# Attention's bias, sinks and first tiles loaded one stage earlier, in an encoder layer on one Trainium2 core

## The chip, the cores and the metric

The kernel runs on one core of one Trainium2 chip. A core has five instruction streams that meet only through semaphores: TensorE (PE, matrix products and transposes), VectorE (DVE), ScalarE (ACT), GpSimd (POOL) and SyncE (SP, which in this kernel issues nearly all DMAs). The metric is the device time of one launch in microseconds (us); lower is better. Three runs of the kernel before gave 1611.4, 1613.11 and 1617.85 us, so the median is 1613.11.

## The reference, cut to what matters

One encoder layer is computed for two token sets that share weights: 1024 sample tokens and 512 prompt tokens, all float32.

```python
h = rmsnorm(x); qa, ka, va, qb, kb, vb = split(h @ w_in)      # 8 heads of 64 in each group, 2 key/value heads
A: s = q.k*scale + bias(rel), |q-k| <= 128; m = max(s, sink); p = exp(s-m)/(sum exp(s-m) + exp(sink-m)); o = p @ v
B: q, k rms-normalised per head and rotated; p = softmax(q.k*scale) over all keys; o = p @ v
x += concat(rmsnorm(oA), rmsnorm(oB)) @ w_out
x += expert_choice_moe(rmsnorm(x)); x += sigmoid(rmsnorm(x) @ w_pg) * (p @ w_pp); y = rmsnorm(x)
```

## The kernel before, in words

The program is a chain of stages, each a block of the five streams: the projection (`project_inputs`), attention on the sample tokens (`attend`, stage name `sample`), attention on the prompt tokens (`attend` again, stage name `prompt`), output product and routing, experts, and the last product. A stage ends when its SP stream has seen its last stores land; then semaphores are cleared and all engines meet at a barrier (`Arena.give_back`, L65-L69). No instruction of a stage is issued before that barrier, so whatever a stage reads from DRAM begins to move only then.

Tokens go in 12 tiles of 128: 8 of the sample, 4 of the prompt. Each float32 operand is held as a high and a low part. The projection writes, for every tile, q (transposed, high and low, 1 MB), k (512 KB) and v (128 KB) to the DRAM arrays `qT_d`, `kT_d` and `v_d` (`store`, L238-L248). `qT` and `kT` in SBUF are single buffers: ACT's `copy_out` of tile t waits until the stores of tile t-1 have landed (L349-L353). Early in the stage `w_raw`, a ring of three, holds raw weights until DVE has made their low parts, and ACT stores the table of relative biases, spread over all partitions, to `rel_d` (L151-L153). SP's order in this stage is written out: x tile t+1 in, q, k, v of tile t-2 out.

`attend` goes through n tiles. In each, PE makes the scores of 16 heads (0 to 7 group A: a span of two or three blocks of keys in `ka`; 8 to 15 group B: all keys of the token set, in `kb`), DVE finds the maxima (in group A it adds `bias` first, L963), ACT takes the exponentials (L909), PE transposes the probabilities (L807) and multiplies with `va` or `vb` (L817). `q`, `ka` and `va` have two slots, by the parity of the tile. PE's head 0 of a tile waits for q, ka and va of its slot (L774-L776), head 8 of the first tile waits for `kb` and `vb` (L777-L778), and DVE begins with `nsinks`, after `bias` and `sinks` have landed (L1031-L1032). An identity matrix for the transposes is made by POOL at the start of each stage (L74-L81), and PE waits for it first. SP's queue after the barrier is

```python
load(0, 0, True, False)                    # q, ka, va of the first tile
if tile0 == 0: consts.load(sp)             # bias 1536 KB, sinks
sp.dma_start(kb[:]...); sp.dma_start(vb[:]...)
load(1, 1, False, False)                   # q, ka, va of the second tile
if tile0 == 0: consts.load_gains(sp)
if w: w.load(sp, w_next, 0, KC // 2)       # prompt stage alone: half of w_out
```

The prompt stage reuses `bias`, `sinks` and the gains `g_mix`, and beside its own work splits `w_out` for the next stage (ACT L103, DVE L107, from head 11 of its first tile on).

Of the kernel before, what the change touches and what calls it, by code (L numbers as in the profile page):

```python
# [6 lines left out]
F32 = mybir.dt.float32  # L7
# [33 lines left out]
class Arena:  # L41
# [7 lines left out]
    def sb(self, name, shape, dt=F32):  # L49
        return self.ctx.enter_context(self.nc.sbuf_tensor(f"{self.stage}_{name}", shape, dt))  # L50
# [20 lines left out]
    def sems(self, name, n):  # L71
        return [self.sem(f"{name}{i}") for i in range(n)]
# [82 lines left out]
def project_inputs(nc, x, w_in, g_attn, gqk, rope, rel_bias, hot, outside, qT_d, kT_d, v_d, rel_d):  # L155
# [3 lines left out]
    with ExitStack() as ctx:  # L159
        a = Arena(nc, ctx, "proj")  # L160
        sb, sem, sems = a.sb, a.sem, a.sems
        w_raw = sb("w_raw", [P, RING, QKV])
        w_hi = sb("w_hi", [P, KC, QKV], F32R)
        w_lo = sb("w_lo", [P, KC, QKV], F32R)
        ident, ident_r = sb("ident", [P, P]), sb("ident_r", [P, P], F32R)
# [28 lines left out]
        p_qk = a.ps("p_qk", [P, 2, 4, P])  # L194
        bias = BiasRows(a)

# [24 lines left out]
        def _(sp):  # L221
# [46 lines left out]
            sp.wait_ge(bias.stored, 16)  # L268
# [302 lines left out]
class AttentionConsts:  # L571


    def __init__(self, nc, kept, rel_d, sink, g_mix):
        self.rel_d, self.sink, self.g_mix = rel_d, sink, g_mix
        tensor = lambda name, shape: kept.ctx.enter_context(nc.sbuf_tensor(name, shape, F32, side="right"))
        self.bias = tensor("bias", [P, HEADS, SPAN])
        self.sinks = tensor("sinks", [P, HEADS])
        self.g_all = tensor("g_mix", [P, 2, HEADS * HD])
        self.landed, self.gains_landed = kept.sem("landed"), kept.sem("gains_landed")  # L580

    def load(self, sp):
# [8 lines left out]
def attend(nc, stage, tile0, n, qT_d, kT_d, v_d, consts, mixed_d, w_next=None, out_w=None):  # L591
# [7 lines left out]
    with ExitStack() as ctx:  # L599
# [3 lines left out]
        bias, sinks, g_all = consts.bias, consts.sinks, consts.g_all  # L603
        nsinks = sb("nsinks", [P, HEADS])
        nhalf = sb("nhalf", [P, 1])
        q_sb = sb("q", [P, 2, 2 * HEADS, P], F32R)
        ka = sb("ka", [P, 2, 2 * KV, SPAN], F32R)
        va = sb("va", [P, 2, 3, KV * HD])
        kb = sb("kb", [P, 2 * KV, T], F32R)
        vb = sb("vb", [P, n, KV * HD])  # L610
# [23 lines left out]
        kb_landed, q_landed, w_landed = sem("kb_landed"), sems("q_landed", 2), sems("w_landed", 2)  # L634
# [57 lines left out]
        def _(sp):  # L692
            tok = tile0 * P

            def load(i, s, first, last):
# [8 lines left out]
                sp.dma_start(q_sb[:, s].bitcast(F32).rearrange("p h q -> p (h q)"), qT_d[src(row, P), :]).then_inc(  # L704
                    q_landed[s], 16)
                start = left + lo * P
                sp.dma_start(ka[:, s, :, lo * P:hi * P].bitcast(F32),
                             kT_d[:, 0:2 * KV, src(start, (hi - lo) * P)]).then_inc(w_landed[s], 16)
                sp.dma_start(va[:, s, lo:hi, :],
# [11 lines left out]
            load(0, 0, True, False)  # L721
            if tile0 == 0:
                consts.load(sp)
            sp.dma_start(kb[:].bitcast(F32), kT_d[:, 2 * KV:, tok:tok + T]).then_inc(kb_landed, 16)
            sp.dma_start(vb[:], v_d[tok:tok + T, 0:KV * HD].rearrange("(b p) d -> p b d", p=P)).then_inc(
                kb_landed, 16)
            load(1, 1, False, False)
            if tile0 == 0:
                consts.load_gains(sp)
# [15 lines left out]
            step(n - 2, 0, last=True)  # L745
            for i in (n - 2, n - 1):
                store(i, A)
                store(i, B)
# [20 lines left out]
        def _(pe):  # L769
            def scores(i, s, head, first, last):  # L770
# [15 lines left out]
                if head < HEADS:  # L786
                    parts = [(slice(lo * P, hi * P), [ka[:, s, 2 * kv + f, lo * P:hi * P] for f in range(2)])]
                else:
                    parts = [(slice(c, c + BANK), [kb[:, 2 * kv + f, c:c + BANK] for f in range(2)])
                             for c in range(0, T, BANK)]  # L790
                for cols, (k_hi, k_lo) in parts:
                    pe.matmul(p_s[:, slot, cols], q_sb[:, s, h, :], k_hi, start=True, stop=False)  # L792
                    made = pe.matmul(p_s[:, slot, cols], q_sb[:, s, h, :], k_lo, start=False, stop=True)  # L793
# [16 lines left out]
            def values(s, g, blocks, begin, end):  # L810


                for b in blocks:
                    for kv in range(KV):
                        v = (va[:, s, b, kv * HD:(kv + 1) * HD] if g == A else vb[:, b, kv * HD:(kv + 1) * HD])
# [134 lines left out]
        def _(dve):  # L950
# [80 lines left out]
            dve.wait_ge(consts.landed, 32)  # L1031
# [5 lines left out]
            dve.wait_ge(consts.gains_landed, 16)  # L1037
# [1100 lines left out]
def encoder_layer(nc, i, y):  # L2138
# [12 lines left out]
    with ExitStack() as ctx:  # L2151
# [4 lines left out]
        project_inputs(nc, i["x"], i["w_in"], i["g_attn"], i["gqk"], i["rope"], i["rel_bias"], i["hot"],  # L2156
                       i["outside"], qT_d, kT_d, v_d, rel_d)
        with ExitStack() as both:
            held = Arena(nc, both, "attend")
            consts = AttentionConsts(nc, held, rel_d, i["sink_a"], i["g_mix"])  # L2160
            attend(nc, "sample", 0, SAMPLE_TILES, qT_d, kT_d, v_d, consts, mixed_d)
# [5 lines left out]
            attend(nc, "prompt", SAMPLE_TILES, TILES - SAMPLE_TILES, qT_d, kT_d, v_d, consts, mixed_d, i["w_out"], out_w)  # L2167
# [60 lines left out]
```

## Time and profile before

| | us |
|---|---|
| median of three runs | 1613.11 |
| the profiled execution | 1608.08 |
| its span, first to last instruction | 1606.3 |
| PE busy | 1442.6 (90% of the span) |
| DVE, ACT, POOL busy | 932.2, 723.0, 182.1 |
| projection's last engine instruction ends; sample stage's first score | 269.8; 282.6 |
| sample stage's last PE work; prompt stage's first score | 560.6; 574.0 |

In the rows, times are in us from the span's start and durations in us, or in ns where a mean is given. A row of a timeline names the start, the duration, the engine, the line, the operation, the tensor written and those read, and in brackets how long the engine was idle before and what ended that. "SPq" rows are DMAs being issued; the bytes move afterwards. PEclk is the clock that TensorE was granted, 1.00 being 2.4 GHz and 0.50 being 1.2 GHz.

### The profile page before, as it was taken

What the parts mean: (1) busy time and instruction counts of PE and PEld (TensorE: products, weight loads), DVE (VectorE), ACT (ScalarE), POOL (GpSimd) and SP (SyncE); (2) the same over time, 40 slices, a digit from 0 to 9 for tenths busy, and PEclk for the clock granted to TensorE, in tenths of its full rate; (3) what the DMA queues carried; (4) which work ended last, traced back from release to release, by engine and by line L of the source; (5) the groups of instructions that cost most, each with busy time, mean ns of one, the idle gap of its engine ahead of it and who ended that gap; (6) DMA issues with size and microseconds to landing.
All of it is one profiled execution on the core that took longest, in us unless ns stands there. A gap on an engine that the chain in (4) does not pass through costs nothing. (4 is left out here: it accounts for less than half of the span.)

```text
span 1606.3 us, 21541 instructions
## 1 busy us (share of the span) xinstructions
PE 1442.6 (90%) x7320; PEld 1015.2 (63%) x7320; DVE 932.2 (58%) x1324; ACT 723.0 (45%) x1157; POOL 182.1 (11%) x255
## 2 busy tenths in 40 slices
PE   5899996799999869689998779999999999938997
PEld 4788885555565445368887556666666666627885
DVE  5454443677777557622257756676676676644553
ACT  4344433666677557522222444544544544423332
POOL 1111110000000000000001211121121121021110
PEclk9899998799999979889998979999999999978998
DMA  8533324621111063064441846778788788753331
GB/s 259 95 112 111 111 98 165 225 71 64 64 64 62 21 236 115 33 220 135 157 144 66 300 164 214 261 261 266 257 259 265 259 261 265 247 158 119 131 132 66
DMA packets 118847, 261.53 MB, mean 163 GB/s; under 512 B 7648, under 2 KB 37472, under 8 KB 115720
## 3 DMA queue, kind: packets, MB, share of 16 engines
q1 hardware_dynamic: 110592, 233.55, 41.4%
q0 software_dynamic: 7168, 25.17, 6.6%
q10 hardware_dynamic: 1032, 2.10, 1.1%
q8 instruction: 32, 0.52, 0.1%
q14 instruction: 23, 0.19, 0.0%
HBM read 194.20 MB, written 66.58 MB: 162 GB/s over the span
## 5 line engine op out<-in xcount | busy, mean ns | idle before, releaser
L1751 DVE TENSOR_TENSOR moe_w_lo<-ring,moe_w_hi 128x2048 fp32r<-128x2048 f32 x96 | 220.3, 2295 | 162.9 <-ACT moe_w_hi L1690 162.9
L1690 ACT ACTIVATE moe_w_hi<-ring 128x2048 fp32r<-128x2048 f32 x96 | 183.7, 1914 | 207.3 <-PE moe_p_g L1873 78.1
L1422 PE MATMUL mix_p_big<-kept_out_w,mix_m_hi 128*128 128x512 f32 x384 | 126.2, 410 | 4.6 <-DVE mix_m_lo L1297 2.4
L519 PE MATMUL proj_p_out<-proj_w_hi,proj_h_hi 128*128 128x512 f32 x264 | 109.8, 416 | 8.4 <-DVE proj_qn L418 8.4
L1881 PE MATMUL moe_p_gu<-ring,moe_xT_r 128*64 128x512 f32 x512 | 116.9, 598 | 0.0
L519 PE MATMUL proj_p_out<-proj_w_lo,proj_h_hi 128*128 128x512 f32 x264 | 105.1, 398 | 0.0
L519 PE MATMUL proj_p_out<-proj_w_hi,proj_h_lo 128*128 128x512 f32 x264 | 104.9, 397 | 0.0
L971 DVE TENSOR_REDUCE sample_ntop<-sample_p_s 128x1 f32<-128x1024 f32 x64 | 78.1, 1222 | 37.9 <-PE sample_p_s L793 37.2
L807 PEld LDWEIGHTS sample_p_t<-sample_ident_r,sample_probs_r 128*128 128x128 f32 x688 | 73.0, 141 | 23.4 <-ACT sample_probs L909 6.7
L1422 PEld LDWEIGHTS mix_p_big<-kept_out_w,mix_m_hi 128*128 128x128 f32 x384 | 72.8, 195 | 21.3 <-issue 2.6
L807 PE MATMUL sample_p_t<-sample_ident_r,sample_probs_r 128*128 128x128 f32 x688 | 80.3, 246 | 5.0 <-ACT sample_probs L909 2.5
L2126 PE MATMUL tail_p_out<-kept_pg_hi,tail_h_hi 128*128 128x512 f32 x192 | 77.5, 404 | 2.4 <-DVE tail_h_lo L2072 2.4
L909 ACT ACTIVATE sample_probs<-sample_p_s,sample_ntop 128x1024 f32<-128x1024 f32 x64 | 71.4, 1116 | 18.1 <-DVE sample_ntop L971 17.7
L1422 PE MATMUL mix_p_big<-kept_out_w,mix_m_lo 128*128 128x512 f32 x192 | 77.6, 404 | 0.0
L2126 PE MATMUL tail_p_out<-kept_pg_hi,tail_h_lo 128*128 128x512 f32 x192 | 76.6, 399 | 0.0
L2126 PE MATMUL tail_p_out<-kept_pg_lo,tail_h_hi 128*128 128x512 f32 x192 | 76.2, 397 | 0.0
L1881 PEld LDWEIGHTS moe_p_gu<-ring,moe_xT_r 128*64 128x64 f32 x512 | 33.9, 136 | 66.1 <-issue 66.1
L792 PE MATMUL sample_p_s<-sample_kb,sample_q 128*128 128x512 f32 x128 | 57.7, 451 | 9.1 <-ACT sample_probs L909 8.6
L817 PE MATMUL sample_p_o<-sample_pT_b,sample_vb 128*64 128x512 f32 x256 | 62.9, 606 | 0.8 <-ACT sample_pT_b L896 0.8
L1649 POOL DMA_INDIRECT acc_d<-ring,kept_slots x32 | 50.5, 1579 | 96.2 <-DVE ring L1792 92.0
L519 PEld LDWEIGHTS proj_p_out<-proj_w_hi,proj_h_hi 128*128 128x128 f32 x264 | 50.0, 189 | 17.8 <-issue 8.5
L909 ACT ACTIVATE sample_probs<-sample_s_a,sample_ntop 128x384 f32<-128x384 f32 (+1 forms) x64 | 37.6, 588 | 46.7 <-DVE sample_ntop L967 45.5
(298 smaller groups left out, 3141.5 us busy)
## 6 DMA issues: line engine op xcount, KB each, us to landing
ring<-in_w_gate SPq DMA_DIRECT2D x32, 1024.0 KB, 5.8
ring<-in_w_up SPq DMA_DIRECT2D x32, 1024.0 KB, 7.6
ring<-in_w_down SPq DMA_DIRECT2D x32, 1024.0 KB, 7.2
qT_d<-proj_qT SPq DMA_DIRECT2D x12, 1024.0 KB, 3.9
sample_q<-qT_d SPq DMA_DIRECT2D x8, 1024.0 KB, 5.1
proj_x<-in_x SPq DMA_DIRECT2D x12, 512.0 KB, 4.3
proj_w_raw<-in_w_in SPq DMA_DIRECT2D x8, 768.0 KB, 5.8
kT_d<-proj_kT SPq DMA_DIRECT2D x12, 512.0 KB, 3.6
```

The source lines that it names most:

```text
L519: last = pe.matmul(p_out[:, cols], h[:, s, k, :], w[:, k, cols], start=(k == 0 and n == 0), stop=(k == KC - 1 and n == 2))
L792: pe.matmul(p_s[:, slot, cols], q_sb[:, s, h, :], k_hi, start=True, stop=False)
L807: last_mm = pe.transpose(p_t[:, bank, b, :].bitcast(F32R), probs_r[:, head % 4, at:at + P], ident_r[:])
L817: mm = pe.matmul(p_o[kv * HD:(kv + 1) * HD, :, :], v, pT[:, b, kv, :, :], start=(b == begin), stop=(b == end - 1))
L909: act.activation(dst, src, ACT.Exp, bias=ntop[:, s, head:head + 1], accum_out=total[:, s, head:head + 1]).then_inc(exp_done, 1)
L971: dve.tensor_reduce(ntop[:, s, head:head + 1], p_s[:, head % 2, 0:T], AX.X, ALU.max, negate=True).then_inc(ntop_done, 1)
L1422: mm = pe.matmul(p_out[:, cols], m[:, s, k, :], ww[:, k, cols], start=(k == 0 and n == 0), stop=(k == KC - 1 and n == 2))
L1649: pool.indirect_dma_start(out=acc_d, out_offset=bass.IndirectOffsetOnAxis(ap=slots[0:rows, col:col + 1], axis=0), in_=y, in_offset=None, c ...
L1690: act.activation(w_hi[:, at % SPLIT], raw[:, at % RAW], ACT.Copy).then_inc(hi_made, 1)
L1751: dve.tensor_tensor(w_lo[:, at % SPLIT], raw[:, at % RAW], w_hi[:, at % SPLIT].bitcast(F32), ALU.subtract).then_inc(lo_made, 1)
L1881: mm = pe.matmul(out[half * R:(half + 1) * R, :], x[:, k0 + k, :], raw[:, (at + half) % RAW, k, :], start=(start and k == 0), stop=(stop a ...
L2126: mm = pe.matmul(p_out[:, s, cols], h[:, s, k, :], ww[:, k, cols], start=(k == 0 and n == 0), stop=(k == KC - 1 and n == 2))
```

## The change

The class `AttentionConsts` becomes `AttentionAhead`. It places `bias`, `sinks`, slot 0 of `ka`, `va` and `q`, the gains, and the prompt's `kb` and `vb` at fixed addresses downward from the top of SBUF. The projection allocates `ident` and the raw weight ring `w_raw` last, so that what lies in the same addresses is what is dead by then. Slot 0 is one buffer shared by both attention stages, slot 1 stays with each stage. What is loaded is the same bytes by the same patterns.

```diff
@@ project_inputs, SP
             load(TILES - 1, 1)
-            for t in range(TILES - 4, TILES):
+            sp.wait_ge(w_lo_made, KC)
+            sp.wait_ge(bias.stored, 16)
+            ahead.load_consts(sp)
+            store(TILES - 4, 0)
+            sp.wait_ge(ident_ready, 1)
+            sp.wait_ge(q_stored, 32)
+            sp.wait_ge(k_stored, 32)
+            for s in range(2):
+                sp.wait_ge(v_stored[s], 16)
+            ahead.load_first(sp, 0)
+            for t in range(TILES - 3, TILES):
                 store(t, t % 2)
@@ AttentionAhead
+    def load_first(self, sp, tile0):
+        row, landed = tile0 * P, self.first_landed[tile0]
+        sp.dma_start(self.q[:].bitcast(F32).rearrange("p h q -> p (h q)"), self.qT_d[row:row + P, :]).then_inc(landed, 16)
+        sp.dma_start(self.ka[:, :, P:3 * P].bitcast(F32), self.kT_d[:, 0:2 * KV, row:row + 2 * P]).then_inc(landed, 16)
+        sp.dma_start(self.va[:, 1:3, :], self.v_d[row:row + 2 * P, KV * HD:].rearrange("(b p) d -> p b d", p=P)).then_inc(
+            landed, 16)
+
+    def load_prompt_keys(self, sp):
+        tok = SAMPLE_TILES * P
+        sp.dma_start(self.kb[:].bitcast(F32), self.kT_d[:, 2 * KV:, tok:]).then_inc(self.kb_landed, 16)
+        sp.dma_start(self.vb[:], self.v_d[tok:, 0:KV * HD].rearrange("(b p) d -> p b d", p=P)).then_inc(
+            self.kb_landed, 16)
@@ attend, SP
-            load(0, 0, True, False)
             if tile0 == 0:
-                consts.load(sp)
-            sp.dma_start(kb[:].bitcast(F32), kT_d[:, 2 * KV:, tok:tok + T]).then_inc(kb_landed, 16)
-            sp.dma_start(vb[:], v_d[tok:tok + T, 0:KV * HD].rearrange("(b p) d -> p b d", p=P)).then_inc(
-                kb_landed, 16)
+                sp.dma_start(kb[:].bitcast(F32), kT_d[:, 2 * KV:, tok:tok + T]).then_inc(kb_landed, 16)
+                sp.dma_start(vb[:], v_d[tok:tok + T, 0:KV * HD].rearrange("(b p) d -> p b d", p=P)).then_inc(
+                    kb_landed, 16)
             load(1, 1, False, False)
@@
             step(n - 2, 0, last=True)
+            if tile0 == 0:
+                sp.wait_ge(qk_done, n * 16 - 16)
+                sp.wait_ge(pv_done[A], n - 1)
+                ahead.load_first(sp, SAMPLE_TILES)
+                ahead.load_prompt_keys(sp)
             for i in (n - 2, n - 1):
                 store(i, A)
@@ attend, PE, scores
-                if head == 0:
-                    pe.wait_ge(q_landed[s], (i - s) * 8 + 16)
-                    pe.wait_ge(w_landed[s], (i - s) * 16 + 32)
+                if head == 0 and first:
+                    pe.wait_ge(ahead.first_landed[tile0], 48)
+                elif head == 0:
+                    pe.wait_ge(q_landed[s], (i - s) * 8 + 16 * s)
+                    pe.wait_ge(w_landed[s], (i - s) * 16 + 32 * s)
```

The first place is SP's queue from the end of the projection into the sample stage. Before, with the row `L159` standing for the stage's end and the next branch for the start of `attend`:

```order
L248 DMA v_d<-proj_v 128x256
L159 UNCONDITIONAL_BRANCH
L691 UNCONDITIONAL_BRANCH
L704 DMA sample_q<-qT_d 128x2048
L707 DMA sample_ka<-kT_d 128x4x256
L709 DMA sample_va<-v_d 128x2x128
L584 DMA bias<-rel_d 128x8x384
L585 DMA sinks<-in_sink_a 128x8
L724 DMA sample_kb<-kT_d 128x4x1024
L725 DMA sample_vb<-v_d 128x8x128
L704 DMA sample_q<-qT_d 128x2048
```

In the changed kernel the same loads stand between the stores of the projection's last four tiles:

```order
L256 DMA proj_x<-in_x 128x1024
L609 DMA ahead_bias<-rel_d 128x8x384
L610 DMA ahead_sinks<-in_sink_a 128x8
L243 DMA qT_d<-proj_qT 128x2048
L246 DMA kT_d<-proj_kT 1024x1x128
L249 DMA v_d<-proj_v 128x256
L619 DMA ahead_q_53<-qT_d 128x2048
L620 DMA ahead_ka_51<-kT_d 128x4x256
L621 DMA ahead_va_52<-v_d 128x2x128
L243 DMA qT_d<-proj_qT 128x2048
```

and the sample stage begins with

```order
L733 UNCONDITIONAL_BRANCH
L764 DMA sample_kb<-kT_d 128x4x1024
L765 DMA sample_vb<-v_d 128x8x128
L746 DMA sample_q<-qT_d 128x2048
L749 DMA sample_ka<-kT_d 128x4x384
L751 DMA sample_va<-v_d 128x3x128
L613 DMA ahead_g_mix<-in_g_mix 128x1024
```

Five loads have moved ahead of the barrier; the sample's `kb` and `vb` now stand first behind it.

The second place is SP's queue from the end of the sample stage into the prompt stage. Before (`L599` is the stage's end, `L691` the start of the next):

```order
L719 DMA mixed_d<-sample_mixedb 128x512
L599 UNCONDITIONAL_BRANCH
L691 UNCONDITIONAL_BRANCH
L704 DMA prompt_q<-qT_d 128x2048
L707 DMA prompt_ka<-kT_d 128x4x256
L709 DMA prompt_va<-v_d 128x2x128
L724 DMA prompt_kb<-kT_d 128x4x512
L725 DMA prompt_vb<-v_d 128x4x128
L704 DMA prompt_q<-qT_d 128x2048
L707 DMA prompt_ka<-kT_d 128x4x384
L709 DMA prompt_va<-v_d 128x3x128
L98 DMA prompt_w_out_raw<-in_w_out 128x1024 x4
```

In the changed kernel, at the end of the sample stage and then at the start of the prompt stage:

```order
L619 DMA ahead_q_53<-qT_d 128x2048
L620 DMA ahead_ka_51<-kT_d 128x4x256
L621 DMA ahead_va_52<-v_d 128x2x128
L626 DMA ahead_kb<-kT_d 128x4x512
L627 DMA ahead_vb<-v_d 128x4x128
L761 DMA mixed_d<-sample_mixeda 128x512
```

```order
L733 UNCONDITIONAL_BRANCH
L746 DMA prompt_q<-qT_d 128x2048
L749 DMA prompt_ka<-kT_d 128x4x384
L751 DMA prompt_va<-v_d 128x3x128
L98 DMA prompt_w_out_raw<-in_w_out 128x1024 x4
```

All five loads that the prompt's first tile reads have moved ahead of the barrier; behind it only the second tile's loads and those of `w_out` are left.

## Rows read from the trace of the kernel before

**Rows 1.** Windows: stretch, length, busy us and count of PE, PEld, DVE, ACT, POOL, PEclk, DMA share, GB/s.

```profile
60.00:262.00 202.00, 201.56 (x1066) 164.66 (x1065) 93.83 (x143) 81.80 (x151) 29.68 (x38) 1.00 0.34 113
262.00:301.00 39.00, 16.51 (x70) 12.81 (x69) 11.70 (x38) 12.71 (x33) 0.82 (x4) 0.56 0.80 281
...
560.00:585.00 25.00, 11.05 (x47) 8.93 (x48) 9.57 (x36) 8.44 (x28) 1.37 (x5) 0.59 0.74 265
```

**Rows 2.** Timeline around the sample stage's start: SP, POOL, PE, DVE, PE.

```profile
275.69 0.35 SPq L704 DMA_DIRECT2D sample_q<-qT_d  x1
...
276.40 0.29 POOL L81 CAST sample_ident_r<-sample_ident 128x128 fp32r<-128x128 f32 x1
...
282.64 0.55 PE L792 MATMUL sample_p_s<-sample_ka,sample_q 128*128 128x256 f32 x1 [13.51 <-DMA sample_va<-v_d]
...
288.11 0.17 DVE L1032 TENSOR_SCALAR sample_nsinks<-sinks 128x8 f32<-128x8 f32 x1 [22.94 <-DMA sinks<-in_sink_a]
...
295.10 0.79 PE L792 MATMUL sample_p_s<-sample_kb,sample_q 128*128 128x512 f32 x1 [0.37 <-DMA sample_vb<-v_d]
```

**Rows 3.** Timeline around the prompt stage's start: SP, DVE, POOL, PE, PE, ACT.

```profile
566.88 0.34 SPq L704 DMA_DIRECT2D prompt_q<-qT_d  x1
...
566.93 0.19 DVE L1032 TENSOR_SCALAR prompt_nsinks<-sinks 128x8 f32<-128x8 f32 x1 [3.30 <-PEq L69]
...
567.61 0.29 POOL L81 CAST prompt_ident_r<-prompt_ident 128x128 fp32r<-128x128 f32 x1
...
574.00 0.55 PE L792 MATMUL prompt_p_s<-prompt_ka,prompt_q 128*128 128x256 f32 x1 [13.46 <-DMA prompt_va<-v_d]
...
580.79 0.76 PE L792 MATMUL prompt_p_s<-prompt_kb,prompt_q 128*128 128x512 f32 x1
...
586.92 1.04 ACT L103 ACTIVATE kept_out_w<-prompt_w_out_raw 128x1024 fp32r<-128x1024 f32 x1
```

**Rows 4.** DMA issues up to 560 us: count, KB each, median us from issue to landing.

```profile
qT_d<-proj_qT SPq DMA_DIRECT2D x12, 1024.0 KB, 3.9
...
sample_kb<-kT_d SPq DMA_DIRECT2D x1, 2048.0 KB, 14.3
...
bias<-rel_d SPq DMA_DIRECT2D x1, 1536.0 KB
...
sample_ka<-kT_d SPq DMA_DIRECT2D x2, 512.0 KB, 6.1
...
sample_vb<-v_d SPq DMA_DIRECT2D x1, 512.0 KB, 14.7
...
sample_va<-v_d SPq DMA_DIRECT2D x2, 128.0 KB, 6.1
```

**Rows 5.** Timelines of SP and ACT around the places of the moved loads.

```profile
205.33 0.83 SPq L255 DMA_DIRECT2D proj_x<-in_x  x1
220.46 0.35 SPq L242 DMA_DIRECT2D qT_d<-proj_qT  x1
...
236.83 1.10 ACT L355 ACTIVATE proj_qT<-proj_p_qk 128x512 fp32r<-128x512 f32 x2
...
518.19 0.36 SPq L719 DMA_DIRECT2D mixed_d<-sample_mixedb  x1
525.73 0.33 SPq L719 DMA_DIRECT2D mixed_d<-sample_mixeda  x1
```

**Rows 6.** Windows of 1 us, PE alone: length, busy time, PEclk, DMA share, GB/s.

```profile
260.00:261.00 1.00, 1.00 (x9) 1.00 0.99 418
...
300.00:301.00 1.00, 1.00 (x3) 0.52 0.52 209
...
584.00:585.00 1.00, 1.00 (x7) 0.87 1.02 406
```

**Rows 7.** Timeline of DVE in the sample stage's first tile: heads 8 and 9.

```profile
297.21 1.23 DVE L971 TENSOR_REDUCE sample_ntop<-sample_p_s 128x1 f32<-128x1024 f32 x1 [1.52 <-PE sample_p_s L793]
...
299.25 1.23 DVE L971 TENSOR_REDUCE sample_ntop<-sample_p_s 128x1 f32<-128x1024 f32 x1 [0.75 <-PE sample_p_s L793]
```

More of the change, by code:

```diff
@@ L569, in _, with __init__, place, reserve @@
             transpose_qk(TILES - 1, False)
[L571 to L582, printed above, removed]
+class AttentionAhead:
+    def __init__(self, nc, held, rel_d, sink, g_mix, qT_d, kT_d, v_d):
+        self.nc, self.rel_d, self.sink, self.g_mix = nc, rel_d, sink, g_mix
+        self.qT_d, self.kT_d, self.v_d = qT_d, kT_d, v_d
+        self.low = nc.sbuf_top
+        self.bias = self.place("bias", [P, HEADS, SPAN])
+        self.sinks = self.place("sinks", [P, HEADS])
+        self.ka = self.place("ka0", [P, 2 * KV, SPAN], F32R)
+        self.va = self.place("va0", [P, 3, KV * HD])
+        self.q = self.place("q0", [P, 2 * HEADS, P], F32R)
+        self.g_all = self.place("g_mix", [P, 2, HEADS * HD])
+        self.kb = self.place("kb", [P, 2 * KV, T_PROMPT], F32R)
+        self.vb = self.place("vb", [P, T_PROMPT // P, KV * HD])
+        self.landed, self.gains_landed, self.kb_landed = (
+            held.sem(n) for n in ("consts_landed", "gains_landed", "prompt_kb_landed"))
+        self.first_landed = {0: held.sem("sample_first_landed"), SAMPLE_TILES: held.sem("prompt_first_landed")}
+    def place(self, name, shape, dt=F32):
+        self.low -= 4 * int(np.prod(shape[1:]))
+        return self.nc.alloc_sbuf_tensor_at(f"ahead_{name}", shape, dt, offset=self.low)
+    def reserve(self, held):
+        held.ctx.enter_context(self.nc.sbuf_tensor("ahead", [P, (self.nc.sbuf_top - self.low) // 4], F32, side="right"))
+    def load_consts(self, sp):
         sp.dma_start(self.bias[:], self.rel_d[:, :, P - 1:P - 1 + SPAN]).then_inc(self.landed, 16)
@@ L602, in attend @@
         ident, ident_r = sb("ident", [P, P]), sb("ident_r", [P, P], F32R)
-        bias, sinks, g_all = consts.bias, consts.sinks, consts.g_all
+        bias, sinks, g_all = ahead.bias, ahead.sinks, ahead.g_all
         nsinks = sb("nsinks", [P, HEADS])
         nhalf = sb("nhalf", [P, 1])
[L606 to L610, printed above, removed]
+        q_sb = [ahead.q, sb("q1", [P, 2 * HEADS, P], F32R)]
+        ka = [ahead.ka, sb("ka1", [P, 2 * KV, SPAN], F32R)]
+        va = [ahead.va, sb("va1", [P, 3, KV * HD])]
+        if tile0 == 0:
+            kb, vb = sb("kb", [P, 2 * KV, T], F32R), sb("vb", [P, n, KV * HD])
+        else:
+            kb, vb = ahead.kb, ahead.vb
         s_a = sb("s_a", [P, 2, SPAN])
@@ L786, in scores @@
                 if head < HEADS:
-                    parts = [(slice(lo * P, hi * P), [ka[:, s, 2 * kv + f, lo * P:hi * P] for f in range(2)])]
+                    parts = [(slice(lo * P, hi * P), [ka[s][:, 2 * kv + f, lo * P:hi * P] for f in range(2)])]
                 else:
@@ L791, in scores @@
                 for cols, (k_hi, k_lo) in parts:
[L792 to L793 removed]
+                    pe.matmul(p_s[:, slot, cols], q_sb[s][:, h, :], k_hi, start=True, stop=False)
+                    made = pe.matmul(p_s[:, slot, cols], q_sb[s][:, h, :], k_lo, start=False, stop=True)
                 made.then_inc(qk_done, 1)
@@ L1029, in tile @@
                         normalise(i - 1, B)
-            dve.wait_ge(consts.landed, 32)
+            dve.wait_ge(ahead.landed, 32)
             dve.tensor_scalar(nsinks[:], sinks[:], -1.0, None, ALU.mult).then_inc(nsink_made, 1)
```

37 lines of the change are left out of this document (20 added, 17 removed).

## The prediction

> **What bounds the kernel now.** I read first the windows by stage. Through the projection's steady part TensorE is busy 201.56 of 202 us, so nothing that feeds it there can gain [rows 1]. Two stretches stand out: 262 to 301 us, with 16.51 us of TensorE work in 39 us, and 560 to 585, with 11.05 in 25; in both the DMA engines are at 0.74 to 0.80 of their time and TensorE's clock averages 0.56 to 0.59 [rows 1]. These are the starts of the two attention stages, and the reader is to see that there the DMA is the busy resource and the engines wait.
>
> Then the timelines of these two stretches, to see which wait ends last. At the sample stage SP comes out of the barrier at 275.69 and issues q, ka, va, bias, sinks, kb, vb. PE begins at 282.64, released by va. DVE can't begin before 288.11, when sinks, the last of the constants, have landed. PE's head 8 comes at 295.10, after 0.37 us of idle that ends with vb [rows 2]. So three waits in a row hang on one queue, and the last, on vb, is the one that sets the pace behind it. At the prompt stage bias is already there, PE's wait of 13.46 us ends with va at 574.00, and from then on nothing waits for the queue: head 8 follows at 580.79 with no idle before it [rows 3].
>
> The whole program is a chain of stages with barriers, so a shift of a stage's first tile passes unchanged to the end, unless something later in the same stage was waiting for a transfer.
>
> **Start of the prompt stage.** q, ka, va, kb and vb of the first tile are issued in the sample stage. What is then late is the identity matrix: POOL's cast begins at 567.61 and takes 0.29, so it is done at 567.90, and PE can begin at about 567.95 in place of 574.00 [rows 3]. That is 6.05 us. The chain of scores, maxima and exponentials behind it is the same instructions in the same order: from the first score to head 8 it takes 580.79 - 574.00 = 6.79 us [rows 3], and kb has landed long before. Could the rest of SP's queue now be late? The second tile's q, ka, va (1024 + 768 + 192 KB by the access patterns) and the first four chunks of w_out (512 KB each) start at once. ACT wants the first chunk at 586.92 - 6.05 = 580.87 [rows 3]; 2496 KB at the rate worked out below need about 8.3 us from 566.9 and are there at about 575.3. So 6.05 stands. Bounds: nothing gained if PE's first scores can't come earlier for another reason; at most 6.05 + 0.5, as no row lets PE pass the identity.
>
> **Start of the sample stage.** Without the loads, PE can begin when the identity is there: cast at 276.40 plus 0.29 gives 276.7 [rows 2]. DVE's constants have landed by then. From first score to head 8 the prompt stage shows 6.79 us with bias at hand and at the same half clock [rows 3], and heads 0 to 7 have the same shapes in both, 128x256. So head 8 is wanted at 276.7 + 6.8 = 283.5. But kb and vb still move only after the barrier, now first in the queue. When do they land? Cumulated from 275.69: q + ka + va = 1664 KB [rows 4] landed by 282.64, that is 6.95 us; with bias and sinks, kb and vb it is 1664 + 1540 + 2560 = 5764 KB by 295.10 [rows 2, 4], so 4100 KB took 12.46 us, 329 KB/us; over the last part alone, 2560 KB from 288.11 to 295.10, it is 366 KB/us. kb + vb are 2560 KB: 6.95 us for the first 1664, and 896 KB more at 329 to 366 take 2.4 to 2.7; together 9.5 us, landing at 285.2. So a wait of 1.7 us for vb takes the place of the three waits, and head 8 starts at 285.2 instead of 295.10: 9.9 us gained. The bounds: if kb and vb keep the times of before, 14.3 and 14.7 from issue to landing [rows 4], with vb issued some 1.3 us after the barrier, head 8 comes at 291.7, a gain of 3.4; if they come in time, it comes at 283.5, a gain of 11.6. I take the value in the middle because in the rows 14.3 and 14.7 contain 3.1 MB of other loads ahead of them in the same queue, which have gone. What stands behind them (the second tile's 1984 KB, the gains) is wanted only a whole tile later, about 20 us after head 0.
>
> The Trainium skill, page "DMA: Bandwidth & Descriptors", section "Anatomy of one DMA — SWDGE (gpsimd) path", gives a transfer as about 2.0 us plus bytes over 436 GB/s. For q + ka + va that is 5.9 us where the row shows 6.95, so the trace is slower than the rule by 1 us. By the rule kb and vb would be there 8.0 us after the barrier, at 283.7, the wait would nearly vanish and the sum would grow by 1.5 us.
>
> **The clock.** TensorE is at 0.50, its level of 1.2 GHz, when both stages begin, and comes back to 2.4 GHz in the window 584 to 585 in the prompt stage (0.87) and 300 to 301 in the sample stage (0.52) [rows 6]. In the prompt stage, where PE runs through, that is 584.26 - 574.00 = 10.3 us after its first score; this shifts with the start and changes nothing. In the sample stage before, PE first had two scores, then stood until DVE began, and the clock came back 5.9 us after head 8's start. By the prompt's row it would now come back at 276.7 + 10.3 = 287.0, 1.8 us after head 8's start: 4.1 us less at half clock, some two heads of group B, which follow each other at 2.04 us on DVE [rows 7], of which DVE's own reduction is 1.23, so 0 to 0.8 us each, 0 to 1.6 in all. If the 1.7 us of waiting starts the count anew, it comes back at 295.5 and the same price is lost instead: -1.6 to 0. I take +0.4, since PE's pause is short beside the work around it.
>
> **What the moved loads cost where they are now.** In the projection bias and sinks (1540 KB) go out after the x load of 205.33 and have the queue until tile 8's q store at 220.46 [rows 5]: 15.1 us for a transfer that took at most 288.11 - 282.64 = 5.5 us after the one ahead of it [rows 2]. q, ka, va of tile 0 follow tile 8's stores. The single q buffer is what could hurt: ACT's first copy of tile 9 at 236.83 waits for tile 8's q store, issued at 220.46 and landed 3.9 us later at 224.4 [rows 4, 5]; so 12.4 us of slack, and only bytes ahead of that store could eat it. The 1664 KB behind it need 7 us and end before tile 9's stores begin. SP's own waits there (low parts made, bias stored, first tiles stored) are for things of the first tiles. PE isn't slowed by traffic: at 418 GB/s it is busy the whole microsecond at clock 1.00 [rows 6]. In the sample stage the five loads go out after the scores of tile 6, about 518.5, right behind the store of 518.19; the next store is at 525.73 [rows 5], and issuing five DMAs takes about 0.5 us each, so it isn't touched. 1664 + 1024 + 256 = 2944 KB are moved in about 9 us, more than 40 us before they are read. Cost: 0, hidden by TensorE's work on both sides; if that cover were gone it would be the 7 to 9 us of the transfers themselves.
>
> **The sum.** 9.9 + 6.05 + 0.4 = 16.35 us. From the profiled execution, 1608.08 (a span of 1606.3 and 1.8 around it), that gives 1591.7. The three runs have their median 5.0 us higher, at 1613.11; taken from there the result is 1596.8, and that is my number.
>
> **Rivals.**
> Rival 1, kb and vb late: they take the time of before although the queue ahead of them is empty (the 4096-byte rows of kb or the issue could be what is slow). For it: the 14.3 us of the row. Against: the cumulated bytes explain it. Gain 3.4 + 6.05 = 9.45, time 1603.7. Still faster.
> Rival 2, no change: the first instructions of PE or ACT in a new stage are not there at the barrier, since their streams have had 13.5 us of waiting in which to get ready, which no row separates from the wait for data. For it: that nothing shows these engines at work sooner. Against: DVE's first instruction starts at 566.93, 0.05 us after SP's [rows 3]. If PE needed until 574.0 and 282.6 anyway, the gain would be 0 at the prompt stage; at the sample stage head 8 would be at 282.64 + 6.8 = 289.4, a gain of 5.7: 1607.4. It counts as no change.
> Rival 3, slower: the added transfers hold up tile 8's q store, ACT waits with its copy, and with it PE, which is busy all the time there. Place: the store at 220.46. It decides once bias takes more than 15.1 + 12.4 = 27.5 us [rows 5]; beyond that each us costs one. To lose 16.35 it has to take 44 us, eight times the 5.5 seen; with 55 us the time would be 1624. Small packets (1536-byte rows) speak for a slower transfer, nothing for this much.
> Rival 4, it does not do what it says: the loads are issued early but wait at SP for something late (a load behind tile 11's stores), and come with the barrier as before: time 1613. The waits name only values reached in the first 60 us.
>
> **How the numbers follow.** Forecast 0.72, rival 1 0.14, rival 2 0.08, rival 3 0.03, rival 4 0.03. A measurement of this kernel tells 0.5%, 8 us, from no change. Forecast and rival 1 lie beyond it, save for their tails (0.03 in all): faster 0.83. Same: rivals 2 and 4 and the tails, 0.13. Slower 0.04. The range: the bounds of the terms give gains of 3.4 + 6.05 - 1.6 = 7.9 to 11.6 + 6.05 + 1.6 = 19.3; from 1613.1 that is 1593.8 to 1605.2. The median of before is itself uncertain by -1.7 to +4.7, and the profiled execution is below it, so I go down to 1591 and stop above at 1604.
>
> **What would show it.** Right: PE's first scores about 1 us after the barrier in both stages; DVE's nsinks at once in the sample stage; one wait of 1 to 3 us on vb before head 8 of its first tile, none in the prompt's; the clock back some 10 us after the first score; the projection's stores at the times of before; the prompt's start 16 us earlier. Wrong: a wait of PE after the barrier that names no DMA (rival 2), vb landing 14 us after its issue (rival 1), or longer idle of ACT before `qT` at tiles 9 and 10 (rival 3).

## The result, and the profile after

The changed kernel takes 1593.14 us (median of four runs, 1592.16 to 1595.72), the kernel before 1612.26 beside it (four runs). The ratio is 0.989, 95% interval 0.9869 to 0.9912: 14 to 21 us less. The profiled execution took 1595.72, with a span of 1593.9; that is 12.4 less than the span of before. The two profiled executions lie at opposite ends of their groups: 1608.08 is below all four times of the kernel before, 1595.72 the highest of the changed kernel's four.

Windows of the changed kernel by stage, columns as in [rows 1]:

```profile
60.00:262.00 202.00, 200.03 (x1049) 163.46 (x1047) 91.29 (x138) 80.13 (x147) 29.41 (x37) 0.99 0.38 125
262.00:301.00 39.00, 26.13 (x133) 20.03 (x132) 20.04 (x52) 19.99 (x46) 0.82 (x4) 0.69 0.62 221
555.00:580.00 25.00, 17.68 (x84) 12.47 (x84) 16.16 (x45) 15.86 (x43) 1.36 (x5) 0.73 0.51 182
```

Against [rows 1], TensorE does 9.6 us more work in the 39 us around the sample stage's start, and DMA's share fell from 0.80 to 0.62. The first row shows something else: TensorE isn't quite full in the projection (200.03 of 202 us).

The sample stage's start, timeline, answering [rows 2]:

```profile
278.36 0.40 SPq L764 DMA_DIRECT2D sample_kb<-kT_d  x1
...
278.42 0.18 DVE L1079 TENSOR_SCALAR sample_nsinks<-ahead_sinks 128x8 f32<-128x8 f32 x1 [10.61 <-PEq L69]
...
279.08 0.29 POOL L81 CAST sample_ident_r<-sample_ident 128x128 fp32r<-128x128 f32 x1
...
279.42 0.58 PE L839 MATMUL sample_p_s<-ahead_ka,ahead_q 128*128 128x256 f32 x1 [7.65 <-POOL sample_ident_r L81]
...
287.95 0.80 PE L839 MATMUL sample_p_s<-sample_kb,ahead_q 128*128 128x512 f32 x1 [1.50 <-DMA sample_vb<-v_d]
```

The barrier's time is taken at POOL's first instruction behind it (278.37 here), which is up to 0.01 us after SP's row. PE begins 1.05 us after the barrier (6.95 before), released by the identity and no longer by a DMA, and DVE works at once. One wait is left: 1.50 us on vb ahead of head 8, which comes 9.58 us after the barrier (19.41 before).

The prompt stage's start, answering [rows 3]:

```profile
559.59 0.34 SPq L746 DMA_DIRECT2D prompt_q<-qT_d  x1
...
560.31 0.29 POOL L81 CAST prompt_ident_r<-prompt_ident 128x128 fp32r<-128x128 f32 x1
...
560.66 0.58 PE L839 MATMUL prompt_p_s<-ahead_ka,ahead_q 128*128 128x256 f32 x1 [7.41 <-POOL prompt_ident_r L81]
...
567.48 0.76 PE L839 MATMUL prompt_p_s<-ahead_kb,ahead_q 128*128 128x512 f32 x1
...
573.63 1.04 ACT L103 ACTIVATE kept_out_w<-prompt_w_out_raw 128x1024 fp32r<-128x1024 f32 x1
```

PE begins 1.07 us after the barrier (7.11 before), and head 8 follows 6.82 us later without a wait.

The moved loads in the projection, SP's queue and then ACT's copy of tile 9, answering [rows 5]:

```profile
208.89 0.61 SPq L609 DMA_DIRECT2D ahead_bias<-rel_d  x1
...
223.09 0.35 SPq L243 DMA_DIRECT2D qT_d<-proj_qT  x1
...
227.79 0.53 SPq L619 DMA_DIRECT2D ahead_q<-qT_d  x1
...
239.47 1.10 ACT L365 ACTIVATE proj_qT<-proj_p_qk 128x512 fp32r<-128x512 f32 x2
```

The store and the copy both come 2.6 us later than in [rows 5], so they moved together: the stage was late before it got there, and its barrier is as late (278.37 against 275.69). The account of the 12.4 us, in spans:

| part | before | changed | difference |
|---|---|---|---|
| start to the sample stage's barrier | 275.69 | 278.37 | +2.68 |
| barrier to head 8 | 19.41 | 9.58 | -9.83 |
| head 8 to the prompt stage's barrier | 271.79 | 271.64 | -0.15 |
| barrier to head 8 | 13.90 | 7.89 | -6.01 |
| head 8 to the end of the prompt stage | 101.21 | 101.62 | +0.41 |
| the rest | 924.30 | 924.80 | +0.50 |

The open questions were whether the two big terms belong to the two halves of the change, where the 2.68 us came from, what the wait on vb and the identity are worth, and how close the moved loads are to doing harm.

### The profile page after: what moved, and what is told of

Same layout as the page of the kernel before. It is cut to its first block and busy times, and to the rows that moved or that the text cites. A ratio compares the mean times of both kernels' runs of the same rounds, so it can differ in the third digit from the quotient of the medians.

```text
span 1593.9 us, 21545 instructions
## 1 busy us (share of the span) xinstructions
PE 1445.4 (91%) x7320; PEld 1017.7 (64%) x7320; DVE 932.5 (59%) x1324; ACT 722.8 (45%) x1157; POOL 182.1 (11%) x255
## 5 line engine op out<-in xcount | busy, mean ns | idle before, releaser
L1469 PEld LDWEIGHTS mix_p_big<-kept_out_w,mix_m_hi 128*128 128x128 f32 x384 | 73.2, 196 | 21.4 <-DVE mix_m_lo L1344 2.6
L956 ACT ACTIVATE sample_probs<-sample_p_s,sample_ntop 128x1024 f32<-128x1024 f32 x64 | 71.4, 1116 | 18.1 <-DVE sample_ntop L1018 17.7
L1928 PE MATMUL moe_p_yr<-ring,moe_hT_r 128*64 128x512 f32 x256 | 58.5, 599 | 0.0
L529 PEld LDWEIGHTS proj_p_out<-proj_w_hi,proj_h_lo 128*128 128x128 f32 x264 | 50.2, 190 | 12.3
```

The costliest lines, as they stand in the source:

```text
L529: last = pe.matmul(p_out[:, cols], h[:, s, k, :], w[:, k, cols], start=(k == 0 and n == 0), stop=(k == KC - 1 and n == 2))
L956: act.activation(dst, src, ACT.Exp, bias=ntop[:, s, head:head + 1], accum_out=total[:, s, head:head + 1]).then_inc(exp_done, 1)
L1469: mm = pe.matmul(p_out[:, cols], m[:, s, k, :], ww[:, k, cols], start=(k == 0 and n == 0), stop=(k == KC - 1 and n == 2))
L1928: mm = pe.matmul(out[half * R:(half + 1) * R, :], x[:, k0 + k, :], raw[:, (at + half) % RAW, k, :], start=(start and k == 0), stop=(stop a ...
```

## The experiments

The ratios are to the kernel before, timed on the same chip.

**Each half of the change alone.** `a1_sample_only` issues the prompt's five loads behind its barrier again, as before:

```diff
@@ attend, SP
+            else:
+                ahead.load_first(sp, tile0)
+                ahead.load_prompt_keys(sp)
             load(1, 1, False, False)
@@
-            if tile0 == 0:
-                sp.wait_ge(qk_done, n * 16 - 16)
-                sp.wait_ge(pv_done[A], n - 1)
-                ahead.load_first(sp, SAMPLE_TILES)
-                ahead.load_prompt_keys(sp)
```

> The changed kernel, with the prompt's first q, ka, va and its kb, vb loaded again behind the barrier. My theory (each stage's start is worth its own wait: 9.8 us at the sample stage, 6.05 at the prompt stage): 6 us slower than the changed kernel, about 1599 against 1593 and 1612 before; the prompt stage's first score about 7.1 us after its barrier, the sample stage's head 8 at 9.6 us after its barrier. Rival (something else in the change, such as where the projection's buffers lie, makes part of the 19 us): the time stays under 1596, as the prompt's part is worth less than 3 us.

`a2_prompt_only` does so with the sample's bias, sinks, q, ka and va:

```diff
@@ project_inputs, SP (and the waits between them)
-            ahead.load_consts(sp)
-            ahead.load_first(sp, 0)
@@ attend, SP
             if tile0 == 0:
+                ahead.load_first(sp, 0)
+                ahead.load_consts(sp)
```

> The changed kernel, with bias, sinks and the sample's first q, ka, va loaded again behind the barrier, ahead of kb and vb. My theory: head 8 of the sample's first tile is back at some 19.4 us after the barrier, and the whole is 10 us slower than the changed kernel, about 1603; the buffers lie as in the changed kernel, so the two undone parts together (this and the run with the prompt's part undone) account for 16 us of the 19 measured, and the rest is spread between executions. Rival (the layout of the buffers gives 3 us by itself): this kernel is at 1603 or below and the sum of the two parts falls short of 16 by more than 2 us.

Measured: 1603.49, ratio 0.9958 (0.9942 to 0.9973), and 1604.66, ratio 0.9975 (0.9961 to 0.9989). PE's rows in `a1_sample_only`: head 8 of the sample, then heads 0 and 8 of the prompt:

```profile
284.85 0.80 PE L837 MATMUL sample_p_s<-sample_kb,ahead_q 128*128 128x512 f32 x1 [1.68 <-DMA sample_vb<-v_d]
...
564.91 0.55 PE L837 MATMUL prompt_p_s<-ahead_ka,ahead_q 128*128 128x256 f32 x1 [13.42 <-DMA ahead_va<-v_d]
...
571.70 0.76 PE L837 MATMUL prompt_p_s<-ahead_kb,ahead_q 128*128 128x512 f32 x1
```

and in `a2_prompt_only`, head 8 of the sample, then head 0 of the prompt:

```profile
296.03 0.80 PE L832 MATMUL sample_p_s<-sample_kb,ahead_q 128*128 128x512 f32 x1 [0.32 <-DMA sample_vb<-v_d]
...
570.14 0.58 PE L832 MATMUL prompt_p_s<-ahead_ka,ahead_q 128*128 128x256 f32 x1 [7.43 <-POOL prompt_ident_r L81]
```

Barrier to head 8 is 9.76 and 13.84 us in the first, 19.82 and 7.89 in the second. Each half gives its own term and leaves the other's as it was. By medians the first half gains 7.0 us and the second 5.9 (from 1610.53), 12.9 together, while the terms make 9.65 and 6.01. The missing 2.7 us lie outside the terms. In the traces, 1.2 us of each kernel's loss stand between head 8 of the sample stage and the prompt's barrier, 273.0 us in place of 271.8, where TensorE's clock falls near the stage's end (see the best version below). Against the changed kernel's 1593.14 both medians are also higher than expected (1603.49 for about 1599, 1604.66 for about 1603). Neither rival's condition was met, so nothing here says that the layout of the buffers gains anything by itself.

**The same two kernels again.** `c1_changed_again` is the changed kernel and `c3_sample_only_again` the first half alone, both unedited.

> The changed kernel itself once more, beside the others of this group. Theory: its trace has the terms of the first one (head 8 at 9.6 us behind the sample stage's barrier, 7.9 behind the prompt's), and 16 to 19 us less than the kernel before. If the first result was lucky in its executions, the gain comes out at 15 to 16 us, the sum of the terms seen in the trace.

> The kernel with the sample stage's part alone, once more beside the changed kernel. Theory: 6 us slower than the changed kernel of this group. Its executions in the last group had their median 4 us above its profiled one, at 1603.5; if that comes back, and is 10 us over the changed kernel, undoing the prompt's part costs more than the 6 us that its trace shows.

Measured: 1594.82, ratio 0.9906 (0.9886 to 0.9927), and 1600.9, ratio 0.9946 (0.9929 to 0.9962): the prompt's half is worth 6.1 us between the two, as its term has it; single executions of the changed kernel spread from 1589.25 to 1598.9, so the closeness is in part luck. But one and the same kernel, the first half alone, had the sample stage's barrier at 275.09 in the first trace and at 280.59 in the second.

**What sets the projection's end.** In every trace that has the projection's x loads and table store as the changed kernel has them (`b3_bias_6x` apart, which delays the projection later on), the sample barrier goes with one instruction, ACT's first square of the fifth x tile (`proj_sq`), which waits for its x. The changed kernel, SP and ACT around it, then PE behind it:

```profile
67.53 6.07 SPq L249 DMA_DIRECT2D v_d<-proj_v  x1
...
73.90 1.07 SPq L256 DMA_DIRECT2D proj_x<-in_x  x1
...
79.13 1.06 ACT L322 ACTIVATE proj_sq<-proj_x 128x1024 bf16<-128x1024 f32 x1 [6.13 <-DMA proj_x<-in_x]
...
81.68 0.66 PE L545 MATMUL proj_p_qk<-proj_ident_r,proj_q_hl 128*128 128x128 f32 x4 [1.97 <-ACT proj_qT L365]
```

and the kernel before:

```profile
67.88 3.94 SPq L248 DMA_DIRECT2D v_d<-proj_v  x1
...
77.93 1.06 ACT L312 ACTIVATE proj_sq<-proj_x 128x1024 bf16<-128x1024 f32 x1 [4.60 <-DMA proj_x<-in_x]
```

SP needs 4 to 6 us to issue one small store of v, the x load is behind it in the queue, and PE waits in its turn: 1.97 us here, 0.44 in the kernel before. In the changed kernel the clock drops with that wait. Three windows of 5 us show it (length, PE's busy us and count, PEclk, DMA share, GB/s), the kernel before, the changed one and `b2_keys_and_identity`, where `proj_sq` is as late (79.42) but PE waits 1.40 us only and keeps its clock:

```profile
80.00:85.00 5.00, 4.56 (x30) 1.00 0.25 105
```

```profile
80.00:85.00 5.00, 3.32 (x14) 0.69 0.00 0
```

```profile
80.00:85.00 5.00, 3.60 (x22) 1.00 0.00 0
```

Over these traces `proj_sq` at 77.33, 77.63, 77.93, 78.36 and 79.42 went with barriers at 275.09, 275.42, 275.69, 276.21 and 277.27 (`a1_sample_only`, `a4_keys_ahead`, before, `a2_prompt_only`, `b2_keys_and_identity`), 197.8 to 197.9 us later each; in all five the clock is 1.00 from 80 to 85. At 79.1 to 79.4 it went with 278.2 to 278.7 (`a3_keys_second`, both traces of the changed kernel, `b3_bias_3x`), and at 80.04 with 280.59 (`c3_sample_only_again`), 199.1 to 200.6 us later, and there the clock is 0.66 to 0.73. So of the changed kernel's 2.68 us some 1.2 are x landing later, and the other 1.5 come on top where the clock dropped. All of this lies ahead of the first moved load at 208.9, and the same kernel stands at both ends of the list, so it isn't the change's doing. My suspect was ACT's spread store of the bias table, 2048 KB that run from 32 to 66 us. `c2_rel_later` moves it:

```diff
@@ project_inputs, ACT
-            bias.store(act, rel_d)          # behind the last chunk of weights
...
             tile(3, 1, False, False)
+            bias.store(act, rel_d)
```

> The changed kernel, with ACT's store of the spread bias rows (2048 KB) issued behind the projection's tile 3 in place of ahead of tile 1. In all traces so far this store runs at some 50 GB/s from 32 to 66 us, SP's issue of tile 0's v store then takes 3.9 to 6.1 us, the x tile behind it is late, and where it lands at 79 us and not at 77 to 78 the projection ends 3 us later. Theory: with the store out of the way the v issue takes under 1 us, x is there in time, and the barrier comes at 272 to 275 us in place of 275 to 278; 1 to 4 us faster than the changed kernel, with less scatter. Rival (the late x is not from this store): the same times as the changed kernel.

It failed: 1615.98, ratio 1.0045 (1.0028 to 1.0062), slower than the kernel before. SP and ACT in its projection:

```profile
115.33 13.43 SPq L249 DMA_DIRECT2D v_d<-proj_v  x1
...
129.05 3.73 SPq L256 DMA_DIRECT2D proj_x<-in_x  x1
...
137.86 1.06 ACT L322 ACTIVATE proj_sq<-proj_x 128x1024 bf16<-128x1024 f32 x1 [16.17 <-DMA proj_x<-in_x]
```

The issue of tile 0's v store fell to 0.36 us, as the suspicion has it, but a later one now took 13.43 us and its x came 16 us late; the barrier moved to 298.35. So the table's store does hold up SP's issues, and in the one other place tried it did more harm. The other way is to give x more cover: `d1_x_earlier` fetches each x one tile sooner.

```diff
@@ project_inputs, SP
+            load(3, 1)
@@ in the loop
-                    load(i * 2 + k + 1, 1 - k)
+                    load(i * 2 + k + 2, k)      # and the stores of tile t-2 behind it
@@
-            load(TILES - 1, 1)
```

> The changed kernel, with each x tile of the projection loaded one tile earlier, ahead of the stores beside which it was issued. The runs so far end the projection at 275 to 281 us, and the late ones are those in which tile 4's x, issued at 72 to 74 us behind tile 0's v store, lands at 79 us or later. Theory: x is never late, the sample stage's barrier opens at 273 to 275 us in the profiled run, and the median is 2 to 4 us below the changed kernel. Rival (the stores of tile 0 themselves, held up by the spread bias rows, are what costs, through the single q buffer): 0 to 1 us below, with the barrier at 275 to 278 as before.

Measured: 1591.57, ratio 0.9885 (0.9863 to 0.9908). The same two instructions:

```profile
67.98 3.74 SPq L249 DMA_DIRECT2D v_d<-proj_v  x1
...
73.27 1.05 ACT L322 ACTIVATE proj_sq<-proj_x 128x1024 bf16<-128x1024 f32 x1
```

The v store still takes 3.74 us to issue, but ACT no longer waits, and the barrier is at 274.84, 3.5 us earlier than in the two traces of the changed kernel; in `d2_all`, which has the same edit, the v store takes 5.13 us and the barrier is at 275.60. That is the 2.68 us of the account, and somewhat more. The ratio's interval overlaps that of the changed kernel, so the median alone doesn't show the gain; the barrier's place in these two traces does.

**The wait on vb.** `a3_keys_second` puts the second tile's loads (1984 KB) ahead of kb and vb again, so that the wait grows by a known number of bytes:

```diff
@@ attend, SP
+            load(1, 1, False, False)
             if tile0 == 0:
                 sp.dma_start(kb[:]...); sp.dma_start(vb[:]...)
-            load(1, 1, False, False)
```

> The changed kernel, with the second tile's q, ka, va (1984 KB) issued ahead of the sample's kb and vb. Theory (head 8 waits for bytes in the queue, at about 366 KB/us): head 8 comes 5.4 us later than in the changed kernel, 15.0 us after the barrier in place of 9.6, and the time is 5 us longer, about 1598. Rival (kb and vb have a duration of their own, and the queue ahead of them matters little): under 2 us longer.

`a4_keys_ahead` takes it away: the projection's g, x, sq and xn buffers are placed with those that die, and kb and vb of the sample stage are loaded into them after tile 9's stores.

```diff
@@ project_inputs, SP
+            store(TILES - 3, 1)
+            sp.wait_ge(squared, TILES); sp.wait_ge(normed, TILES); sp.wait_ge(xT_made, TILES)
+            ...                             # q, k, v of all sample tiles stored
+            ahead.load_sample_keys(sp)
-            for t in range(TILES - 3, TILES):
+            for t in range(TILES - 2, TILES):
```

> The changed kernel, with the sample's kb and vb loaded in the projection as well, behind tile 9's stores, into the place of x, its square, its norm and the gains, all dead by then. Theory: the wait of 1.5 us before head 8 goes, head 8 comes about 8.0 us after the barrier, and the time is 1.5 to 2 us shorter, 1591 to 1592. On the clock: if the pause of PE before head 8 puts off its return to 2.4 GHz, then it now comes back 10 us after the first score, as at the prompt's start, in place of 14; if it hangs on the work that PE does, then about 5.5 us after head 8 begins in any case.

Measured: `a3_keys_second` 1600.5, ratio 0.9929 (0.9908 to 0.995), `a4_keys_ahead` 1590.76, ratio 0.9887 (0.9866 to 0.9908). PE's head 8 in the first:

```profile
292.92 0.80 PE L839 MATMUL sample_p_s<-sample_kb,ahead_q 128*128 128x512 f32 x1 [6.67 <-DMA sample_vb<-v_d]
```

14.76 us after the barrier in place of 9.58, so 1984 KB ahead in the queue cost 5.18 us. In `a4_keys_ahead` head 8 comes after 7.88 us without a wait, exactly as in the prompt stage.

**The identity.** `b2_keys_and_identity` adds to that one identity for all three stages, kept from the projection on:

```diff
@@ attend
-            make_identity(pool, ident, ident_r, cleared, ident_ready)
-            pe.wait_ge(ident_ready, 1)
```

> The changed kernel with the sample's kb and vb loaded in the projection, and with the projection's identity matrix kept for both attention stages, so that PE waits for nothing after the barrier. Theory: PE's first score 0.1 to 0.2 us after the barrier in both stages in place of 1.05, head 8 at about 7 us in both; 1.7 + 2 x 0.9 = 3.5 us faster than the changed kernel. Rival (PE's first instructions of a stage are not ready at the barrier): the first score still comes about 1 us behind it.

Measured: 1590.22, ratio 0.9889 (0.9867 to 0.991). SP's first DMA and PE's first score:

```profile
277.27 0.35 SPq L772 DMA_DIRECT2D sample_q<-qT_d  x1
...
277.31 0.55 PE L860 MATMUL sample_p_s<-ahead_ka,ahead_q 128*128 128x256 f32 x1 [6.63 <-PEq L69]
```

PE begins 0.03 us behind the barrier: nothing but data held it there. Head 8 follows at 6.83 in both stages.

**The moved loads made heavier.** Bias and sinks are loaded three and six times in a row, each copy after the one before has landed:

```diff
@@ project_inputs, SP (b3_bias_3x; 6 in b3_bias_6x)
-            ahead.load_consts(sp)
+            for r in range(3):
+                sp.wait_ge(ahead.landed, 32 * r)
+                ahead.load_consts(sp)
```

> The changed kernel, with bias and sinks loaded three times over in the projection, each after the last has landed, ahead of tile 8's stores. Theory (the moved loads have 15.1 us of free queue and 12.4 us more before ACT wants tile 8's q store landed): some 20 to 24 us, tile 8's q store goes out at about 230 in place of 223 us, and nothing is lost: the stores of tiles 9 to 11 and the barrier are where they are in the changed kernel. Rival (a late store costs at once): 7 us longer.

> The same six times over. Theory: at 7 us each the last lands at about 251, tile 8's q store goes out then and lands at 255, 15 us behind ACT's first copy of tile 9 at 239.5; the projection ends 12 to 18 us later, and the time is as much longer than the changed kernel's. Rival (the queue isn't on the path in any case): no loss.

Measured, one execution each: 1595.97 and 1617.25. With three, tile 8's q store goes out at 226.89 and the barrier is at 278.70, within 0.4 us of the changed kernel's. With six, SP and ACT:

```profile
248.01 0.54 SPq L611 DMA_DIRECT2D ahead_bias<-rel_d  x1
...
249.39 0.35 SPq L243 DMA_DIRECT2D qT_d<-proj_qT  x1
...
260.81 1.08 ACT L367 ACTIVATE proj_qT<-proj_p_qk 128x512 fp32r<-128x512 f32 x2
```

The copy is 21.3 us later than in the changed kernel, PE waits 20.4 us for it, and the barrier comes 23.5 us later, where 12 to 18 were expected. The store is 26.3 us late and, with the last copy of bias still ahead of it, takes 11.4 us to the ACT copy that waits for its landing, in place of 3.9 [rows 4]: 26.3 + 7.5 less the slack of 12.4 is 21.4 us. The slack was right; the store's own landing behind a full queue was what I hadn't counted.

**The best version.** `d2_all` joins `b2_keys_and_identity` and `d1_x_earlier`.

> The version with the sample's kb and vb in the projection, the identity kept and x one tile earlier. Theory, from the terms: 2.8 us (head 8 of the sample stage) + 1.1 us (of the prompt stage) + 2 to 4 us (x) below the changed kernel, about 1587 to 1589, 1.3 to 1.4% below the kernel before.

Measured: 1587.84 (1586.45 to 1590.49), ratio 0.9858 (0.9836 to 0.9881), the fastest of all. Its first score and the last of its two heads 8:

```profile
275.65 0.55 PE L860 MATMUL sample_p_s<-ahead_ka,ahead_q 128*128 128x256 f32 x1 [6.59 <-PEq L69]
...
563.68 0.76 PE L860 MATMUL prompt_p_s<-ahead_kb,ahead_q 128*128 128x512 f32 x1
```

Head 8 starts 6.83 and 6.82 us behind the two barriers. Part of what it gains is lost again at the end of the sample stage, where the clock falls. PE's 32 products with `vb` of the last heads there, in the changed kernel:

```profile
544.93 7.09 PE L864 MATMUL sample_p_o<-sample_pT_b,sample_vb 128*64 128x512 f32 x32 [0.83 <-ACT sample_pT_b L943]
```

and in `d2_all`:

```profile
539.31 9.50 PE L885 MATMUL sample_p_o<-sample_pT_b,ahead_vb_s 128*64 128x512 f32 x32 [0.83 <-ACT sample_pT_b L963]
```

`a4_keys_ahead`, where they take 8.78 us, shows why in windows of 1 us, PE alone, columns as in [rows 6]:

```profile
539.00:540.00 1.00, 0.18 (x2) 0.94 0.24 80
540.00:541.00 1.00, 1.00 (x4) 0.50 0.00 0
...
543.00:544.00 1.00, 1.00 (x6) 0.85 0.40 152
```

The clock is at 0.50, 1.2 GHz, from 540 on and back within 543. The products take 7.09 us in the kernel before, in both traces of the changed kernel, in `d1_x_earlier` and in both kernels with heavier loads, which need 271.6 to 272.1 us from head 8 to the prompt's barrier, and 8.70 to 10.03 us in the eight others, which need 272.9 to 274.4. It isn't the stage's own work: `c2_rel_later` has the changed kernel's sample stage to the letter and takes 8.78. What decides it is open.

## Why the prediction was right

Forecast 1596.8, range 1591 to 1604; measured 1593.14. The mechanism held step by step.

- **Prompt stage, 6.05 us: measured 6.01.** PE was released by POOL's cast, 0.06 us after its end; head 8 followed after 6.82 us (6.79 forecast); ACT's first `w_out` chunk came with no wait on its load.
- **Sample stage, 9.9 us: measured 9.83.** The forecast had head 8 wait for vb until 9.5 us after the barrier, 1.7 us of it idle; it waited 1.50 us, until 9.58. The way it was worked out, cumulated bytes over the rate of the same queue, was tried on a second amount by `a3_keys_second`: 5.18 us for 1984 KB, where 5.4 was expected.
- The rule of the Trainium skill ("DMA: Bandwidth & Descriptors", "Anatomy of one DMA — SWDGE (gpsimd) path"), 2.0 us plus bytes over 436 GB/s, would have made it 8.0 us; the trace has 9.58. That is no test of the rule itself, since the section fits it to single transfers on GpSimd's path, and these are two loads issued one behind the other by SP. As `a4_keys_ahead` has PE ready for head 8 at 7.88, nearly the whole wait is the difference between rule and rows.
- **Clock, +0.4 us: the step that was wrong in its working.** I took the clock to return 10.3 us after the first score, as it does where PE runs through. In the changed kernel's sample stage it returned 14.1 us after it, 5.6 after head 8's start. The first row is from there, the second, where it comes 9.3 us after the first score, from the prompt stage:

```profile
293.00:294.00 1.00, 1.00 (x4) 0.75 0.43 168
...
569.00:570.00 1.00, 1.00 (x4) 0.51 1.05 418
```

  In `a4_keys_ahead`, without the wait on vb, it was 10.8 us, and in `a3_keys_second`, with 6.67 us of wait, 18.1. The other traces divide the same way: 11.7 to 15.0 us in all eight with a wait of 1.45 to 1.68 us, 9.2 to 10.8 in the three without one, and 7.8 to 10.7 in all prompt stages. So the pause does put it off, which I had named and set aside "since PE's pause is short". The price is small all the same: from the barrier to the first store of the sample stage's results the changed kernel takes 36.84 us and `a4_keys_ahead` 34.76, 2.08 apart, of which head 8 is 1.70. That leaves 0.4 us for the clock. The +0.4 us of the forecast, a gain over the kernel before, came out as 0.15 at most: head 8 to the next barrier took 0.15 us less.
- **Moved loads, 0: right.** With three times the bytes nothing is lost; with six times tile 8's q store goes out 26 us later and PE waits 20.4 us. The transfers themselves were sized too short, though, and only the slack hid it: bias took 7.8 us from issue to landing and sinks, the last of the two, landed 9.4 us after bias's issue (at most 5.5 forecast, from its increment behind other loads), the five loads at the end of the sample stage took 11.9 us (about 9 forecast), and the first chunk of `w_out` landed 8.9 us after the prompt's barrier (some 8.3 forecast, though the forecast's own rates give 9.2 to 9.5), 5.1 us before ACT used it.
- **The sum.** The two terms are 15.84 us. The profiled pair shows only 12.4, since the projection's end was 2.68 us later in the changed kernel's trace. The same spread, 275.1 to 280.6 over executions, is in no term of the prediction and is larger than its clock term. The two comparisons of medians give 19.1 us (1612.26 to 1593.14) and 14.6 (1609.43 to 1594.82). The 3.7 us by which the forecast was high lie within this scatter; no term accounts for them. How near the forecast comes also hangs on where it starts, and that is in part luck: from the profiled 1608.08 the same sum gives 1591.7, from the 1613.11 of three executions 1596.8. The later groups put the kernel before at 1610.53, 1609.43 and 1608.88 (18, 11 and 7 executions), below the start that was taken.

**The rivals.** Rival 1 (kb and vb late in themselves) is refuted: vb landed 9.58 us after the barrier, and later only with bytes ahead of it. Rival 2 (streams not ready) is refuted by 1.05 us in the change and 0.03 in `b2_keys_and_identity`. Rival 3's place and its slack of 12.4 us were right: the store 3.8 us late costs nothing (three times the bytes), 26.3 us late it costs over 20; only the price beyond the point was low, as the store also lands later. Rival 4 is refuted by the issue at 208.89.

## What to carry to other kernels

A stage boundary costs the time from the barrier to the landing of the bytes that the first instructions need; read it as a distance from the barrier in both traces, since the barrier's own place scatters. Load ahead what fits into dead buffers, and then look for the next in line: here vb (1.7 us) and the identity (1.0 us per stage). When a median doesn't add up to its terms, find the part that is not in any term, here an x load queued behind a store that took SP up to 6 us to issue, and give that load a lead; moving what disturbed it cost 21 us in the one place tried.

## What the hardware showed that I had not expected

- A store on another queue can hold up SP's own issues. While ACT's spread store of 2048 KB was under way (32 to 66 us, some 60 GB/s), and just behind it, issuing a store of v took SP 3.7 to 6.3 us, against 0.36 with that store moved away, and 13.43 us where the two met later.
- An engine's first instruction behind a barrier starts at once where its data are there: PE's first score came 0.03 us behind it in `b2_keys_and_identity`.
- TensorE's clock can fall for 3.4 to 6.8 us near the end of a stage (0.50 from 540 to 543 in `a4_keys_ahead`) in kernels that do the same work there, and the same 32 products then take 8.7 to 10.0 us and not 7.09.
- A pause of TensorE of only 1.45 to 1.68 us, while its clock is still at 1.2 GHz, goes with a later return to 2.4 GHz: 11.7 to 15.0 us after the first score, against 9.2 to 10.8 without the pause.
